# Turning normed activations by DMA transposes on SyncE's queue instead of TensorE, in a hybrid decoder block

## What is computed

```python
h = concatenate([meta, x], axis=1)
u = rms_norm(h, norm_mix_g) @ w_in                  # 1024 -> 2576
c_val, c_gate, q, k, v, g, gate_lr = split(u)
y_conv = silu(layer_norm(causal_conv31(c_val * sigmoid(c_gate)) + conv_b))
y_gla  = rms_norm_per_head(gated_linear_attention(q, k, v, gate_lr)) * silu(g)
h = h + concatenate([y_conv, y_gla]) @ w_out        # 1024 -> 1024
n = rms_norm(h, norm_ffn_g)
h = h + (silu(n @ w_gate) * (n @ w_up)) @ w_down    # 1024 -> 2816 -> 1024
out = rms_norm(h, norm_final_g)[:, 16:]
```

## Time and profile before

| what | value |
|---|---|
| median of 3 runs | 1622.52 us (1621.08 to 1630.65) |
| the profiled execution: its own time | 1623.4 us |
| the profiled execution: span of core 0 | 1621.9 us |
| spans of the 8 cores | 1586.4 to 1621.9 us |
| TensorE (PE) busy | 1486.0 us, 92% of the span |
| VectorE (DVE), ScalarE (ACT), GpSimd (POOL) busy | 49%, 35%, 14% |

### The profile page before, as it was taken

One profiled execution on the slowest core, in us unless ns is written; L12 is line 12 of the kernel. 1 busy time (PEld: TensorE's weight loads), 2 busy tenths in 40 slices (PEclk: granted clock), 3 DMA queues, 4 the chain that ended last, 5 costly groups with the idle time before them and its releaser, 6 DMA issues.

```text
span 1621.9 us, 26409 instructions; the slowest of 8 cores (1586.4 to 1621.9 us)
## 1 busy us (share of the span) xinstructions
PE 1486.0 (92%) x8292; PEld 697.4 (43%) x8450; DVE 801.8 (49%) x1779; ACT 563.6 (35%) x865; POOL 219.8 (14%) x323
## 2 busy tenths in 40 slices
PE   4847999989999899998999989999899979999997
PEld 2423444434444344443444434444444434444443
DVE  5446436554365644555355643555435554365533
ACT  4343343223522344133442334423353233523111
POOL 3211124110320103100030000301012010300000
PEclk9978999999999999999999999999999999999999
DMA  9965998887776664347634556347463474444642
GB/s 179 287 169 123 209 209 182 193 242 208 200 187 186 212 185 131 130 157 217 183 124 143 187 178 172 119 148 220 156 168 135 151 233 145 133 155 143 208 143 91
DMA packets 80375, 281.52 MB, mean 174 GB/s; under 512 B 10848, under 2 KB 11232, under 8 KB 80240
## 3 DMA queue, kind: packets, MB, share of 16 engines
q1 hardware_dynamic: 54816, 191.01, 37.7%
q0 software_dynamic: 24048, 87.11, 22.1%
q10 hardware_dynamic: 1376, 1.71, 0.3%
HBM read 252.58 MB, written 41.94 MB: 182 GB/s over the span
## 4 chain that ended last, share of the span: by engine, by line
PE 78%; DMA 8%; issue 6%; DVE 5%; ACT 2%; ACTq 0%; DVEq 0%; POOL 0%; SPq 0%; POOLq 0%
PE ps L620 52%; PE ps L1215 16%; DMA h<-xin 5%; PE ps L826 4%; DMA out<-h 2%; PE ps L611 2%; DMA wring<-wpack 1%; PE ps L704 1%; DVE xn_tm L599 1%; DVE stn L571 1%; DVE h L1279 1%; PE ps L1120 0%; PE ps L1084 0%; PE ps L1089 0%; DVE stn L573 0%
## 5 line engine op out<-in xcount | busy, mean ns | idle before, releaser
L620 PE MATMUL ps<-x2T,wring 128*128 128x512 bf16 x2734 | 635.6, 385 | 23.8 <-DVE h L1223 6.6
L620 PEld LDWEIGHTS ps<-x2T,wring 128*128 128x128 bf16 x2816 | 272.9, 99 | 361.9 <-issue 57.3
L1215 PE MATMUL ps<-wring,actT 128*128 128x512 bf16 x1290 | 292.6, 379 | 7.9 <-DVE U L1041 5.2
L1197 DVE SCALAR_TENSOR_TENSOR ftmp<-ftmp,ps 128x512 f32<-128x512 f32 x176 | 120.0, 685 | 242.8 <-ACT ftmp L1196 240.4
L1196 ACT ACTIVATE ftmp<-ps 128x512 f32<-128x512 f32 x176 | 104.5, 594 | 264.1 <-PE ps L620 241.3
L1215 PEld LDWEIGHTS ps<-wring,actT 128*128 128x128 bf16 x1320 | 126.9, 98 | 151.7 <-issue 7.8
L620 PE MATMUL ps<-xT,wring 128*128 128x512 bf16 x719 | 161.0, 379 | 1.0
L1199 DVE SCALAR_TENSOR_TENSOR actT<-ftmp,ps 128x512 bf16<-128x512 f32 x176 | 120.2, 686 | 54.5 <-PE ps L620 50.7
L620 PE MATMUL ps<-wring,yT 128*128 128x512 bf16 x497 | 116.4, 383 | 1.3 <-ACT yT L1123 0.5
L596 ACT ACTIVATE xn_tm<-h 128x1024 bf16<-128x1024 f32 x64 | 67.5, 1054 | 143.2 <-DVE h L1163 99.7
L620 PEld LDWEIGHTS ps<-xT,wring 128*128 128x128 bf16 x736 | 71.7, 98 | 85.8
(11 more groups left out here) (183 smaller groups left out, 1318.9 us busy)
## 6 DMA issues: line engine op xcount, KB each, us to landing
wring<-wsc SPq DMA_DIRECT2D x322, 512.0 KB, 4.2
wring<-wpack POOLq DMA_DIRECT2D x56, 512.0 KB, 7.6
wsc<-wring POOLq DMA_DIRECT2D x42, 512.0 KB, 6.6
rep<-vT SPq DMA_DIRECT2D x112, 136.1 KB, 6.1
h<-xin POOLq DMA_DIRECT2D x28, 512.0 KB, 12.3
out<-h POOLq DMA_DIRECT2D x28, 512.0 KB, 8.3
h<-xin SPq DMA_DIRECT2D x4, 512.0 KB, 9.8
h<-wpack POOLq DMA_DIRECT2D x4, 512.0 KB, 9.3
```

What stands on the lines that cost most here:

```text
L620: ins = e.matmul(pt_ap, lhsT=lhs(kc), rhs=rhs(kc), start=(kc == 0), stop=(kc == KC - 1))
L1197: P.add("dve", lambda e: e.scalar_tensor_tensor(out=th[:], in0=th[:], scalar=1.0, in1=pg[:], op0=ALU.add, op1=ALU.mult), R=[Bpg, Bth], W=[ ...
L1215: ins = e.matmul(ps[t][:], lhsT=actT[:, j, t * 128:(t + 1) * 128], rhs=wd3[:, j - 4 * s_, :], start=(j == 0), stop=(j == NJ - 1))
```

## The change

From the second block on (wherever `meta` is false) the norm's output tile is turned by one DMA transpose from `xn_tm[i]` straight into `xT` or `x2T`, issued by SyncE; the 8 TensorE transposes, their PSUM bank and ScalarE's copy are gone there. The first block keeps `transp`. The estimate of such a DMA for the order of work is a queue cost of 1.3, and its bytes as those of any transfer. Nothing else changes in the source; the order of all engines' instructions is made anew from the estimates.

```diff
@@ Meter @@
-            if name == "dma_start":
+            if name == "dma_start_transpose":
+                self.nbytes += n * o.shape[0] * 2
+                self.cost += 1.3
+            elif name == "dma_start":
@@ after transp @@
+            def turn(i, dst, Bdst):
+
+                P.add("sp", lambda e: e.dma_start_transpose(out=dst, in_=xn_tm[i][:]), R=[Bxn[i]], W=[Bdst], dkey=f"turn{i}")
+
@@ mixer, tiles of xT (L661) @@
-                        transp(xni[t], xT[:, :, t * 128:(t + 1) * 128], BxT[t])
+                        (transp if meta else turn)(xni[t], xT[:, :, t * 128:(t + 1) * 128], BxT[t])
@@ mixer, tiles 0 and 1 of x2T (L1168) @@
-                                transp(xni2[t - 2], x2T[:, :, (t - 2) * 128:(t - 1) * 128], Bx2T[t - 2])
+                                (transp if meta else turn)(xni2[t - 2], x2T[:, :, (t - 2) * 128:(t - 1) * 128], Bx2T[t - 2])
@@ mixer, tiles 2 and 3 of x2T (L1174) @@
-                        transp(xni2[t], x2T[:, :, t * 128:(t + 1) * 128], Bx2T[t])
+                        (transp if meta else turn)(xni2[t], x2T[:, :, t * 128:(t + 1) * 128], Bx2T[t])
```

## The result

The changed kernel took 1649.7 us (median of 4 runs, against 1621.8 for the kernel before beside it): 1.0149 of the time before, interval 1.011 to 1.0188. So it is slower by 1.5%, where 1598 us, 1.5% faster, was forecast. In the profile taken with that result all eight cores ran at about 0.85 of the clock, so the profile shown here is that of a second execution of the unaltered changed kernel, the run `e1_after_again`.

What follows compares the result with a forecast made beforehand. TensorE, busy 1486.0 of 1621.9 us, was taken as the bound. Six fronts (17.4), seven ends (5.6) and 1.8 us gave 24.8 us gained, so 1598 us; range from 1573, and 3 for the groups, at the low end to 1653.

Steps and rivals of the forecast that it cites:

- Removed work: 56 transpose slots of 0.45 us on TensorE, 25 us; ScalarE's 56 copies counted at nothing except where they end a chain.
- L: Time from the end of a norm's last step to its DMA transpose's landing, taken as 4.5 us.
- The front: Start of six mixers, up to `xT`: gain 11.9 - 2L each, 2.9 us, with two more FFN groups done early.
- The end: Mixer's end, seven times, up to `x2T`: gain the lesser of 1.8 us and 5.3 - L, so 0.8.
- The second block's front and the third block: Second's front: four slots alone, 1.8 us gained; third's front: one of six equal ones, 2.9 us each.
- SyncE's order: Transposes waiting for norms hold weight loads and `rep<-vT` in SyncE's queue: taken as nothing, up to 14 us uncovered; rival's chance 0.04.
- The sum: Six fronts, seven ends and 1.8 us: 110.3 - 19L, at L = 4.5 a gain of 24.8 us.
- The rivals: Faster still, L under 3.5 (0.12); no change, L 5.0 to 6.6 (0.26); slow pieces (0.20); slower by SyncE (0.04).
- slow pieces: Transposes set by their many small pieces, not bytes; decides from L = 6.6, 1664 us at L = 8; chance 0.20.

Runs made afterwards that it cites:

- e1: The changed kernel run once more, unaltered, for a profile at the usual clock; 1.0117 of the kernel before.
- e5: The changed kernel with the planner's price of one `rep<-vT` issue raised from 0.4 to 0.9 us; 0.9964 of the kernel before.
- e3: The changed kernel with DMA transposes for `x2T` alone, `xT` turned by TensorE as before; 1.0011 of the kernel before.
- e7: The changed kernel with DMA transposes from the fourth block on only, second and third turned by TensorE; 1.0126 of the kernel before.
- e8: The changed kernel with `rep<-vT` priced at 0.9 us and DMA transposes only from the fourth block on; 0.9887 of the kernel before.

## Why the prediction was wrong

The steps, in the prediction's order.

**Removed work: right.** The first block's 72 transposes are the only ones left on TensorE (L614), and ScalarE has 56 instructions fewer (809 against 865), 54 us less busy, worth nothing by themselves.

**L: right.** Taken 4.5, measured 4.2 in the median from the norm's end and 4.0 from issue to landing. Of the two readings of the Trainium skill in the prediction, the trace is near the one of Advanced Engine Details and Errata (X-Bar Transpose (TRN2)), which calls transposes as fast as regular DMAs: a transpose takes 4.0 us to land, a weight load with twice its bytes 4.5, though a store of the same bytes takes 2.1. The other, eight times the 1309 ns that the Trainium skill's page VectorE: DVE Perf Modes (The three transpose paths) gives for one block, is not borne out: a whole tile holds the queue for 1.25 us and lands after 4.0.

**The front: the step that failed.** The prediction put it so: "I estimate two more groups of 8 products (none to four) [...] They are work done early, 3.5 us." It was five groups, outside my bounds; that would have made the front's gain larger, and the prediction says so of this case. By its own measure the front did gain: in the fourth block the first `xT` product came 53.4 us after the block's start instead of 51.0, with 8.6 us more of FFN work done by then, so 6.2 us, where 2.9 was forecast. What was false is that work done early is gained; the wait that it uncovers was a term the sum didn't have. The 32 products of it that had stood between `xT` and the convolution were the cover of the copies `rep<-vT`. Without them TensorE stopped there for 4.2 us in the mean of the five steady blocks and lost up to 2.8 us more in the 64 products after it (3.66 before, 5.02 to 6.43 after the stop). I had asked what hides the transposes, and not what the work that hides them had hidden until then. e5 shows the size: give the cover back from elsewhere, and a steady block gains 6.7 us against the kernel before on the slowest core, 2.8 in the median of the eight, where 3.7 was forecast (2.9 and 0.8).

**The end: the wait right, the gain not shown.** Waits of 2.1 to 3.4 us stand at the steady blocks' first products with `x2T`, near the forecast (about 2). For the gain, where I had 0.8 us a block, e3 has 3.0 on the slowest core and nothing in the median of the cores.

**The second block's front and the third block: wrong.** I counted the second's front at 1.8 us gained and the third as one of six equal fronts. They lost 16.3 us together. I priced the transposes at one L for all blocks and showed no row of the early ones. In e1 the `xT` transposes of 345 to 420 us took 6.5 us in the median. Over the eight cores they take 6.3 in the two early periods and 3.9 in the later ones, while the weight loads beside them land hardly later than before (from `wsc` 5.7 before and 6.2, f32 weights 7.5 and 7.6). TensorE waited 12.3 us for f32 weights over the span, 1.9 before. The experiments show that the loss goes when these blocks keep TensorE's transposes (e7, e8); which transfer delays which stays open.

**SyncE's order: right in the steady blocks.** The queue still waits for TensorE most of the time (831.2 us), and TensorE's only wait for weights from `wsc` in e1's steady blocks is one of 1.1 us (0.5 to 5.8 in all on the eight cores).

**The sum.** Forecast 24.8 us gained. By e1's trace it is 19.1 lost. Of the 43.9 between them 22.6 lie in the early blocks (1.8 + 2.9 + 2 x 0.8 = 6.3 forecast as gain, 16.3 lost) and 19.4 in the five steady periods (5 x 3.7 = 18.5 forecast, 0.9 lost). The other 1.9 is ahead of them and behind. The forecast was made from the rows of one core, the one with the longest steady period of the eight; in the median of the cores the steady periods lose 17 us and the early ones 14.

**The rivals.** None of the four is it. The two slower ones were "slow pieces" (L over 6.6) and SyncE's order; L is 4.0, and the order cost little. The measured time, 1649.7, lies within the range (1570 to 1653), but as the range's upper end was made by L it holds it by chance. One of the signs that I gave for being wrong came true, "a first `xT` product with much more FFN work ahead of it than two groups"; I had its consequence the wrong way round.

## What to carry to other kernels

When a planner fills a new, longer latency with independent work, ask where this work stood before and what it covered there: the same products can't hide two waits, and here the second one (16 copies, 10.8 us in a queue) cost at least what the first had gained. A price that is right for the new operation has to be matched by right prices for its neighbours; the copies at 0.4 us against a measured 0.67 were harmless until the spare work between them and their user was gone. And a DMA instead of a compute instruction should go where DMA is idle: with the convolution covered (e5) the same edit gained in the steady blocks and lost in the early ones, and e8 (0.9887) keeps the one without the other. Last, read all cores of a profile: the slowest one alone hid that the steady blocks lost too.

## What the runs showed of the hardware that I had not expected

A DMA transpose of one 128x1024 bf16 tile holds SyncE's queue for 1.25 us (up to 2.02), against 0.32 for a weight load's issue, and lands after 3.0 us at best. It is cheap in time and dear in packets: the span's count rose from 80375 to 139509, and those under 512 B from 10848 to 69984, which is 1056 for each of the 56 transposes. The median landing of the weight loads moved from 4.2 to 4.5 us all the same.

A stop of TensorE is paid twice here. Behind the 3.24 us stop in the fourth block of e1 the granted clock was 0.73 from 627 to 631 us (a part of them at 1.2 of 2.4 GHz) where it had been 1.00 from 611 to 620, and after stops of 3.2 to 5.6 us 64 products took 5.0 to 6.4 us instead of 3.66. With 1.01 us of wait, in the third block of e1, they took 3.65.
